# Grouped-query attention of block 2: the score tiles of two heads in turn, scored together on two halves of TensorE's rows

## The chip, the cores and the metric

The kernel runs on one core of a Trainium2 chip, in float32. The metric is the device time of one execution in microseconds (us). The kernel before took 2878.69 us (median of 3 runs, 2877.79 to 2880.61).

## The reference

Two transformer blocks run one after the other, on 512 tokens of width 1024; the second also has 256 context tokens. The change touches one attention of block 2: eight query heads of width 64 that share two heads of keys and values. Cut to what matters:

```
qb = rmsnorm(gq.reshape(lead + (GQA_HEADS, GQA_DIM)), qg_gain)        # 8 heads of 64
kb = rmsnorm(gk.reshape(lead + (GQA_KV_HEADS, GQA_DIM)), kg_gain)     # 2 heads of 64
...
def joint_dense_attention(q, k, v, kc, vc):       # the 512 tokens attend to context and tokens
    kk = jnp.concatenate([kc, k], axis=1)
    vv = jnp.concatenate([vc, v], axis=1)
    def block(qi):
        sc = jnp.einsum('bqkgd,bnkd->bkgqn', qi, kk) * (d ** -0.5)
        p = jax.nn.softmax(sc, axis=-1)
        return jnp.einsum('bkgqn,bnkd->bqkgd', p, vv)
```

The 256 context tokens attend among themselves in the same manner.

## The kernel before

The program is written engine by engine, with semaphores placed by hand, and falls into stages between which all engines meet. The stage of this change holds the grouped-query attention and, as a *filler* between its steps, the projections, norms and rotations of the first four heads of the latent attention (`pe_latent`, `dve_latent`, `act_latent`), which the next stage needs. The order on each engine is the order in which `pe_attention`, `dve_attention` and `act_attention` write it; no scheduler moves anything.

`dense(8, ...)` (L2464) makes the work list. A *unit* is one score tile: 128 queries of one head against all the keys it sees. Heads go in four couples (2m, 2m+1). For each couple there is a *main* group of 8 units (four query tiles of the first head, then four of the second, 768 keys each) and a *late* group of 4 units (two context tiles of each head, 256 keys each): 48 units in the stage, 32 of them main. Queries of an even head lie on partitions 0 to 63 of `QT`, those of an odd head on 64 to 127, and the keys lie on both halves of `KT`.

One unit x runs through the engines so:

- TensorE `score(x)` (L2331): one matmul of 512 keys and one of 256 into the double bank `PP[x % 2]`, with 64 rows. In float32 every matmul stands in the trace as two records with a weight load each. It waits until the exponential of unit x-2 has read that bank.
- VectorE `soften(x)` (L2386, L2391): the row maximum over 768 (or 256) columns, and its negative.
- ScalarE `exponentials(x)` (L2436): the exponential with the row sum, from `PP[x % 2]` into `PB`.
- VectorE `scale(x)` (L2402, L2404): the reciprocal of the sum, and the product with it.
- TensorE `turn_probs(x)` (L222): six (or two) transposes of 128x128 into `PP[2]`, which is one buffer: it waits until ScalarE has copied unit x-1 out of it.
- ScalarE `copy_probs(x)` (L2446): the copy from `PP[2]` to SBUF.
- When a group's probabilities are all there, TensorE `values` (L2352) makes the products with the values, two heads at once on the two halves of the array's columns, and VectorE (L2411) multiplies the gate by them. `Heads` (L2301) hands these products out two at a time to later units (`A.sums`).

TensorE's loop has score(x+1), a filler step, the values due at x, turn_probs(x-1), a filler step. So the score of the next unit is under way while VectorE and ScalarE work on this one. VectorE has soften(x+1), filler, scale(x), filler; ScalarE has exponentials(x), filler, copy_probs(x-1), filler. A filler step is one item of `latent_order`, in the same order on all engines: for each token tile a product of 384 columns (`q`) and one of 512 (`kv`), both into the one bank `PS[7]`, a square root on ScalarE with two loads of its function table for each two tiles, then many small steps of norm and rotation on VectorE, and four transposes of 96 for q and for k.

Of the kernel before, what the change touches and what calls it, by code (L numbers as in the profile page):

```python
# [95 lines left out]
def emit(nc, D, out, ctx):  # L96
# [13 lines left out]
    PP = [ctx.enter_context(nc.psum_tensor(f"ps{i}", [128, 1024], F32)) for i in range(4)]  # L110
# [44 lines left out]
    pe, dve, act, pool = [count(n + "_step") for n in ("pe", "dve", "act", "pool")]  # L155
# [4 lines left out]
    done, bank, read = {}, {}, {}  # L160
# [79 lines left out]
    class Block:  # L240


        def __init__(self, col, *parts, again=False, kept=False):
            self.col, self.parts = col, parts

            self.again, self.kept = again, kept
# [75 lines left out]
    ab = kp(D["ab_w_in_2"][0])  # L322
# [669 lines left out]
    def steps(filler, n=1):  # L992
        for _ in range(n):
            next(filler, None)
# [1056 lines left out]
    def whole(filler):  # L2051
        for _ in filler:
            pass
# [247 lines left out]
    class Heads:  # L2301


        def __init__(self, tag, groups, rate):
            self.tag, self.groups, self.units = tag, groups, []
            for g, grp in enumerate(groups):
                for n, u in enumerate(grp[0]):
                    self.units.append((g, n == len(grp[0]) - 1) + u)
            self.sums = {}
            todo = []  # L2310
            for x, u in enumerate(self.units):

                self.sums[x], todo = todo[:rate], todo[rate:]
                if x and self.units[x - 1][1]:
                    todo += self.of(x - 1)
            self.sums["end"] = todo + self.of(len(self.units) - 1)
# [5 lines left out]
    def pe_attention(e, A, PB, filler, rate):  # L2322
        exped, scaled, copied, taken_ = [signal(n) for n in ("exped", "scaled", "probs_copied", "values_taken")]
        units = A.units

        def score(x):
            g, end, q, ks = units[x][:4]
            if x >= 2:
                e.wait_ge(*exped.at(x - 1))
            for k, at in ks:  # L2330
                m = e.matmul(PP[x % 2][:, at:at + k.shape[1]], q, k, start=True, stop=True)  # L2331
            m.then_inc(*pe.up())
            done[A.tag, "score", x] = pe.now()

        def turn_probs(x):
            n = units[x][5]
            e.wait_ge(*scaled.at(x + 1))
            if x:
                e.wait_ge(*copied.at(x))
            transposes(e, [(PP[2][:, k * 128:k * 128 + 128], PB[:, x % 2, k * 128:k * 128 + 128]) for k in range(n // 128)]).then_inc(*pe.up())  # L2340
            done[A.tag, "turn", x] = pe.now()

        def values(sums):

            for g, j, x, k, v, c0, c1 in sums:
                bufs, vals = A.groups[g][1], A.groups[g][2]
                if j == 0:
                    e.wait_ge(*copied.at(x + 1))
                    if g:
                        e.wait_ge(*taken_.at(g))  # L2350
                for a in range(2):
                    m = e.matmul(PS[6][64 * a:64 * a + 64, c0:c1], v[a], bufs[a][:, k, c0:c1], start=(j == 0), stop=(j == len(vals) - 1))  # L2352
                if j == len(vals) - 1:
                    m.then_inc(*pe.up())
                    done[A.tag, "values", g] = pe.now()

        score(0)
        for x in range(len(units)):
            if x + 1 < len(units):
                score(x + 1)  # L2360
            steps(filler, rate)
            values(A.sums[x])
            if x:
                turn_probs(x - 1)
            steps(filler, rate)
        turn_probs(len(units) - 1)
        values(A.sums["end"])
        whole(filler)

    def dve_attention(e, A, PB, filler, rate):  # L2370
        units = A.units

        def masks(x):
            p = PP[x % 2]
            for n, (m, at) in enumerate(units[x][6]):
                e.wait_ge(*(dve.now() if n else done[A.tag, "score", x]))
                e.tensor_tensor(p[:, at:at + 128], p[:, at:at + 128], m, ALU.add).then_inc(*dve.up())  # L2377

        def soften(x):
            lo, n, sink = units[x][4], units[x][5], units[x][7]  # L2380
            m = sb[:, x % 2 * 8:x % 2 * 8 + 8]
            e.wait_ge(*done[A.tag, "score", x])
            e.wait_ge(*dve.now())
            if x >= 2:
                e.wait_ge(*signal("scaled").at(x - 1))
            e.tensor_reduce(m[:, 0:1], PP[x % 2][:, lo:lo + n], AX.X, ALU.max).then_inc(*dve.up())  # L2386
            e.wait_ge(*dve.now())
            if sink is not None:
                e.tensor_scalar(m[:, 0:1], m[:, 0:1], sink, -1.0, ALU.max, ALU.mult).then_inc(*dve.up())
            else:  # L2390
                e.tensor_scalar(m[:, 0:1], m[:, 0:1], -1.0, None, ALU.mult).then_inc(*dve.up())  # L2391
            done[A.tag, "max", x] = dve.now()

        def scale(x):
            n, sink = units[x][5], units[x][7]
            m = sb[:, x % 2 * 8:x % 2 * 8 + 8]
            e.wait_ge(*signal("exped").at(x + 1))
            if sink is not None:
                e.wait_ge(*signal("sunk").at(x + 1))
                e.tensor_tensor(m[:, 1:2], m[:, 1:2], m[:, 2:3], ALU.add).then_inc(*dve.up())  # L2400
                e.wait_ge(*dve.now())
            e.reciprocal(m[:, 3:4], m[:, 1:2]).then_inc(*dve.up())  # L2402
            e.wait_ge(*dve.now())
            e.tensor_scalar(PB[:, x % 2, 0:n], PB[:, x % 2, 0:n], m[:, 3:4], None, ALU.mult).then_inc(*signal("scaled").up())  # L2404

        def values(sums):
            for g, j, x, k, v, c0, c1 in sums:
                if j == len(A.groups[g][2]) - 1:
                    n, dst = A.groups[g][3], A.groups[g][4]
                    e.wait_ge(*done[A.tag, "values", g])  # L2410
                    e.tensor_tensor(dst, dst, PS[6][:, 0:n], ALU.mult).then_inc(*signal("values_taken").up())  # L2411

        masks(0)
        soften(0)
        for x in range(len(units)):

            if x + 1 < len(units):
                masks(x + 1)
                soften(x + 1)
            steps(filler, rate)  # L2420
            scale(x)
            values(A.sums[x])
            steps(filler, rate)
        values(A.sums["end"])
        whole(filler)

    def act_attention(e, A, PB, filler, rate):
        units = A.units

        def exponentials(x):  # L2430
            lo, n, sink = units[x][4], units[x][5], units[x][7]
            m = sb[:, x % 2 * 8:x % 2 * 8 + 8]
            e.wait_ge(*done[A.tag, "max", x])
            if x >= 2:
                e.wait_ge(*done[A.tag, "turn", x - 2])
            e.activation(PB[:, x % 2, 0:n], PP[x % 2][:, lo:lo + n], ACT.Exp, bias=m[:, 0:1], accum_out=m[:, 1:2]).then_inc(*signal("exped").up())  # L2436
            if sink is not None:
                e.activation(m[:, 2:3], m[:, 0:1], ACT.Exp, bias=sink).then_inc(*signal("sunk").up())

        def copy_probs(x):  # L2440
            g, end, c, places, a = units[x][0], units[x][1], units[x][8], units[x][9], units[x][10]
            e.wait_ge(*done[A.tag, "turn", x])
            if g >= 2:
                e.wait_ge(*done[A.tag, "values", g - 2])
            for k0, k1, to in places:
                m = e.activation(A.groups[g][1][a][:, to:to + k1 - k0, c * 128:c * 128 + 128],  # L2446
                                 PP[2][:, k0 * 128:k1 * 128].rearrange("p (k n) -> p k n", n=128), ACT.Copy)
            m.then_inc(*signal("probs_copied").up())

        for x in range(len(units)):  # L2450
            exponentials(x)
            steps(filler, rate)
            if x:
                copy_probs(x - 1)
            steps(filler, rate)
        copy_probs(len(units) - 1)
        whole(filler)
# [150 lines left out]
    def pool_latent(e, hh):  # L2608
        for what, i in latent_order():
            if what == "kv":  # L2610
                if i >= 2:
# [2 lines left out]
                              KR[:, i, :].unsqueeze(1).to_broadcast([128, 4, 32])).then_inc(*signal("kr_copied").up())  # L2614

    gqa = Heads("gqa", dense(8, lambda h: QT[half(h), h // 2, :], lambda h: KT[half(h), h // 4, :],
                             lambda h, k: GKV[:, k, 128 + 64 * (h // 4):192 + 64 * (h // 4)], 4), 2)
    pe_attention(nc.tensor, gqa, PB, pe_latent(nc.tensor, 0), 1)
    dve_attention(nc.vector, gqa, PB, dve_latent(nc.vector, 0), 1)
    act_attention(nc.scalar, gqa, PB, act_latent(nc.scalar, 0), 1)  # L2620
# [257 lines left out]
```

## Time and profile before

| | |
|---|---|
| Time, median of 3 runs | 2878.69 us (2877.79 to 2880.61) |
| The profiled execution: its own time, its span | 2879.6 us, 2878.4 us |
| TensorE matmul busy | 2589.5 us, 90% of the span |
| VectorE, ScalarE busy | 995.8 us (35%), 562.5 us (20%) |
| Granted TensorE clock, mean over the span | 0.94 |
| The stage of the change | 2073.6 to 2256.1 us, 182.5 us |
| in it: TensorE, VectorE, ScalarE busy | 169.25, 112.64, 91.15 us |
| in it: granted clock, DMA share | 0.84, 0.00 |

Times are from the start of the span. Busy times of matmuls are a little too long, since a record runs on past the start of the next one; what TensorE needs for a piece is read from the start of its first matmul to the start of the next piece. A clock of 1.00 is 2.4 GHz and 0.50 is 1.2 GHz; no other level occurs. "Idle before" names the engine and line whose signal ended the idle time.

### The profile page before, as it was taken

Reading aid. Unit: us, or ns where it says so; the run is one execution under the profiler, and the core shown is the slowest. Engines: PE = TensorE matmul, PEld = TensorE weight load, DVE = VectorE, ACT = ScalarE, POOL = GpSimd, SP = SyncE. Lnnn points to the kernel's source line nnn. Section 1 sums busy time; section 2 is a strip of 40 time slices with the busy share of each in tenths; the row PEclk is TensorE's granted clock in tenths of the full one; section 3 lists DMA queues with packets and bytes.
Section 4 is the critical chain, followed back from the end, with each engine's and each line's share of the span. In section 5 each row is a group of like instructions: output and inputs, shape, how many; then the busy total and the mean of one; then the engine's idle time right before and its main releaser. Section 6 shows DMA issues by size and latency. Waiting matters only on the chain. (4 is left out here: it accounts for less than half of the span.)

```text
span 2878.4 us, 27051 instructions
## 1 busy us (share of the span) xinstructions
PE 2589.5 (90%) x10307; PEld 1262.8 (44%) x10307; DVE 995.8 (35%) x2127; ACT 562.5 (20%) x1274; POOL 170.0 (6%) x316
## 2 busy tenths in 40 slices
PE   5979778875999999999999999798999789999998
PEld 2534646342334334444343333365544444454453
DVE  2665344333121111111121111345066665332272
ACT  1355322010000000000000000121255544210250
POOL 0000514101000000000000000200000000000000
PEclk8999999976999999999999999899988999999889
DMA  9110185605899999958948999810000002022000
GB/s 324 63 59 30 60 327 180 267 33 195 361 401 414 416 404 417 414 229 323 382 186 354 411 419 417 324 59 26 29 1 1 1 1 81 19 84 86 31 1 29
DMA packets 143354, 565.43 MB, mean 196 GB/s; under 512 B 15429, under 2 KB 36158, under 8 KB 105202
## 3 DMA queue, kind: packets, MB, share of 16 engines
q1 hardware_dynamic: 127336, 515.97, 45.7%
q0 software_dynamic: 12992, 42.51, 3.9%
q10 hardware_dynamic: 2890, 5.13, 0.5%
q8 instruction: 85, 1.39, 0.2%
q14 instruction: 51, 0.42, 0.0%
HBM read 537.24 MB, written 26.35 MB: 196 GB/s over the span
## 5 line engine op out<-in xcount | busy, mean ns | idle before, releaser
L1585 PE MATMUL ps<-ring,mem 128*32 128x512 f32 (+2 forms) x1888 | 517.8, 603 | 10.4 <-issue 10.4
L216 PE MATMUL ps<-ring,mem 128*128 128x512 f32 (+5 forms) x1136 | 398.1, 508 | 29.9 <-DVEq L181 15.0
L216 PE MATMUL ps<-mem,ring 128*128 128x512 f32 (+1 forms) x1056 | 422.0, 559 | 2.6 <-DVE mem L736 1.6
L1585 PEld LDWEIGHTS ps<-ring,mem 128*32 128x32 f32 (+2 forms) x1888 | 189.9, 147 | 278.1 <-issue 278.1
L216 PEld LDWEIGHTS ps<-ring,mem 128*128 128x128 f32 x1136 | 202.9, 197 | 210.2 <-issue 178.8
L216 PEld LDWEIGHTS ps<-mem,ring 128*128 128x128 f32 x1056 | 201.5, 192 | 213.1 <-issue 204.4
L1614 PE MATMUL ps<-ring,mem 128*32 128x512 f32 (+2 forms) x1056 | 270.5, 603 | 9.2 <-issue 9.2
L222 PE MATMUL ps<-mem 128*128 128x128 f32 (+3 forms) x1203 | 193.5, 294 | 85.2 <-DMA mem<-h_rows,mem 14.2
L222 PEld LDWEIGHTS ps<-mem 128*128 128x128 f32 (+3 forms) x1203 | 145.5, 148 | 210.5 <-issue 138.2
L1585 PE MATMUL ps<-mem 128*32 128x512 f32 (+2 forms) x800 | 234.8, 596 | 2.4 <-issue 2.4
L1646 DVE COPY mem<-ps 128x512 f32<-128x512 f32 x48 | 33.2, 692 | 505.9 <-PE ps L222 505.9
L1654 ACT ACTIVATE mem<-mem 128x512 f32<-128x512 f32 x48 | 28.1, 632 | 784.2 <-DVE mem L1630 784.2
L1622 DVE COPY mem<-ps 128x512 f32<-128x512 f32 x48 | 33.3, 693 | 410.8 <-PE ps L222 410.8
L1614 PEld LDWEIGHTS ps<-ring,mem 128*32 128x32 f32 (+2 forms) x1056 | 99.8, 141 | 155.3 <-issue 155.3
L2331 PE MATMUL ps<-ring 64*128 64x256 f32 (+4 forms) x328 | 133.7, 531 | 14.8 <-ACT mem L2436 4.6
L2386 DVE TENSOR_REDUCE mem<-ps 128x1 f32<-128x768 f32 (+3 forms) x128 | 99.1, 774 | 132.3 <-PE ps L2331 125.4
L1585 PEld LDWEIGHTS ps<-mem 128*32 128x32 f32 (+2 forms) x800 | 84.1, 145 | 108.7 <-issue 108.7
L1614 PE MATMUL ps<-mem 128*128 128x512 f32 (+2 forms) x288 | 122.1, 604 | 0.0
L2446 ACT ACTIVATE ring<-ps 128x768 f32<-128x768 f32 (+2 forms) x128 | 75.4, 602 | 121.7 <-PE ps L222 121.5
L2099 ACT ACTIVATE mem<-ps 128x512 f32<-128x512 f32 (+2 forms) x68 | 33.0, 487 | 329.5 <-PE ps L216 329.5
L2331 PEld LDWEIGHTS ps<-ring 64*128 64x128 f32 (+1 forms) x328 | 62.9, 215 | 64.6 <-issue 51.0
L1661 ACT ACTIVATE mem<-ps 128x512 f32<-128x512 f32 x48 | 26.1, 595 | 294.0 <-PE ps L1614 294.0
(374 smaller groups left out, 2373.9 us busy)
## 6 DMA issues: line engine op xcount, KB each, us to landing
ring<-in_w_up SPq DMA_DIRECT2D x91, 2048.0 KB, 15.9
ring<-in_w_down SPq DMA_DIRECT2D x47, 2048.0 KB, 22.4
mem<-in_w_up SPq DMA_DIRECT2D x37, 2048.0 KB, 18.3
mem<-in_w_down SPq DMA_DIRECT2D x17, 2048.0 KB, 20.6
ring<-in_w_ada SPq DMA_DIRECT2D x12, 2048.0 KB, 7.5
ring<-in_mod_w SPq DMA_DIRECT2D x8, 2048.0 KB, 10.4
ring<-in_cd_w_in SPq DMA_DIRECT2D x6, 2048.0 KB, 7.9
y_rows<-mem POOLq DMA_DIRECT2D x23, 512.0 KB, 8.0
```

The lines of the kernel that those rows point to most:

```text
L216: i = e.matmul(o, l, r, start=(n == 0), stop=(n == len(pairs) - 1))
L222: r = e.transpose(o, i, ident[0:k, 0:k])
L1585: m = e.matmul(PS[n][c0:c0 + rows, :], XGT[:, u, k * 128 + c0:k * 128 + c0 + rows], wt[:, kk, n * 512:n * 512 + 512], start=False, stop=(k ...
L1614: m = e.matmul(PS[6 + n][c0:c0 + rows, :], ACTT[:, k * 128 + c0:k * 128 + c0 + rows], wt[:, kk, n * 512:n * 512 + 512], start=False, stop= ...
L1622: e.tensor_copy(XGT[:, i % 2, hh * 512:hh * 512 + 512], PS[4]).then_inc(L.x_copied, 1)
L1646: e.tensor_copy(ACTT[:, hh * 512:hh * 512 + 512], PS[5]).then_inc(L.a_copied, 1)
L1654: e.activation(SG[:, c], T1[:, c], ACT.Sigmoid, scale=1.702).then_inc(L.gate, 1)
L1661: e.activation(Y[:, i % 2, n * 512:n * 512 + 512], PS[6 + n], ACT.Copy).then_inc(L.y_copied, 1)
L2099: e.activation(dst, bank[key][:, 0:n], func).then_inc(*empties(key))
L2331: m = e.matmul(PP[x % 2][:, at:at + k.shape[1]], q, k, start=True, stop=True)
L2386: e.tensor_reduce(m[:, 0:1], PP[x % 2][:, lo:lo + n], AX.X, ALU.max).then_inc(*dve.up())
L2446: m = e.activation(A.groups[g][1][a][:, to:to + k1 - k0, c * 128:c * 128 + 128], PP[2][:, k0 * 128:k1 * 128].rearrange("p (k n) -> p k n", ...
```

## The change

The units of a group are put in another order for this one attention (`side_by_side=True`, in block 2's grouped-query stage alone): first head's tile 0, second head's tile 0, first head's tile 1, and so on. Each loop then takes two units, a *pair*, at a time: 24 pairs, 16 of main units and 8 of late ones. TensorE scores both units of a pair together, one on rows 0 to 63 into `PP[0]` and one on rows 64 to 127 into `PP[1]`, once the exponentials of both units of the pair before are done. VectorE makes both maxima; ScalarE makes both exponentials. No instruction is added or removed; each engine still takes four filler steps for two units. The other attentions keep their loops.

```diff
+        def __init__(self, tag, groups, rate, side_by_side=False):
...
+                if side_by_side:
+                    us = [u for ab in zip(us[:half], us[half:]) for u in ab]
@@ pe_attention @@
+        def scores(x):
+            if x:
+                e.wait_ge(*exped.at(x))
+            for (k0, at), (k1, _) in zip(units[x][3], units[x + 1][3]):
+                e.matmul(PP[0][:, at:at + k0.shape[1]], units[x][2], k0, start=True, stop=True)
+                m = e.matmul(PP[1][:, at:at + k1.shape[1]], units[x + 1][2], k1, start=True, stop=True)
+            m.then_inc(*pe.up())
+            done[A.tag, "score", x] = done[A.tag, "score", x + 1] = pe.now()
+
+        if A.side_by_side:
+            for x in range(0, len(units), 2):
+                scores(x)
+                if x:
+                    turn_probs(x - 2)
+                steps(filler, rate)
+                values(A.sums[x])
+                steps(filler, rate)
+                if x:
+                    turn_probs(x - 1)
+                steps(filler, rate)
+                values(A.sums[x + 1])
+                steps(filler, rate)
@@ dve_attention @@
+        if A.side_by_side:
+            for x in range(0, len(units), 2):
+                for u in (x, x + 1):
+                    masks(u)
+                    soften(u)
+                steps(filler, rate)
+                scale(x)
+                values(A.sums[x])
+                steps(filler, rate)
+                scale(x + 1)
+                values(A.sums[x + 1])
+                steps(filler, 2 * rate)
@@ act_attention @@
+        if A.side_by_side:
+            for x in range(0, len(units), 2):
+                if x:
+                    copy_probs(x - 2)
+                steps(filler, rate)
+                exponentials(x)
+                steps(filler, rate)
+                exponentials(x + 1)
+                steps(filler, rate)
+                if x:
+                    copy_probs(x - 1)
+                steps(filler, rate)
```

How this moves instructions, at three places. First TensorE in main units of the first group with no filler product between them (the score line is L2331 before and L2365, L2366 after; L222 are the transposes). Before:

```order
L2331 MATMUL ps<-ring 128x512
L2331 MATMUL ps<-ring 128x256
L222 MATMUL ps<-mem 128x128 x6
L2331 MATMUL ps<-ring 128x512
L2331 MATMUL ps<-ring 128x256
L222 MATMUL ps<-mem 128x128 x6
```

After:

```order
L2365 MATMUL ps<-ring 128x512
L2366 MATMUL ps<-ring 128x512
L2365 MATMUL ps<-ring 128x256
L2366 MATMUL ps<-ring 128x256
L222 MATMUL ps<-mem 128x128 x12
```

Scores and transposes took turns unit by unit; now four score matmuls stand together, the two heads in turn, and then the twelve transposes of the pair before.

VectorE where the second pair begins, with the maximum (L2386, now L2417), its negative (L2391, L2422), the reciprocal (L2402, L2433), the product (L2404, L2435) and, as filler, the mean (L2561, L2623), its inverse (L2565, L2627) and two steps of a norm (L2027, L2030). Before:

```order
L2386 TENSOR_REDUCE mem<-ps 128x1
L2391 TENSOR_SCALAR mem<-mem 128x1
L2561 TENSOR_SCALAR mem<-mem 128x16
L2402 RECIPROCAL mem<-mem 128x1
L2404 TENSOR_SCALAR mem<-mem 128x768
L2565 RECIPROCAL mem<-mem 128x16
L2027 TENSOR_TENSOR mem<-mem 128x384
L2386 TENSOR_REDUCE mem<-ps 128x1
L2391 TENSOR_SCALAR mem<-mem 128x1
L2030 SCALAR_TENSOR_TENSOR mem<-mem 128x384
L2402 RECIPROCAL mem<-mem 128x1
L2404 TENSOR_SCALAR mem<-mem 128x768
```

After:

```order
L2417 TENSOR_REDUCE mem<-ps 128x1
L2422 TENSOR_SCALAR mem<-mem 128x1
L2417 TENSOR_REDUCE mem<-ps 128x1
L2422 TENSOR_SCALAR mem<-mem 128x1
L2623 TENSOR_SCALAR mem<-mem 128x16
L2433 RECIPROCAL mem<-mem 128x1
L2435 TENSOR_SCALAR mem<-mem 128x768
L2627 RECIPROCAL mem<-mem 128x16
L2027 TENSOR_TENSOR mem<-mem 128x384
L2433 RECIPROCAL mem<-mem 128x1
L2435 TENSOR_SCALAR mem<-mem 128x768
L2030 SCALAR_TENSOR_TENSOR mem<-mem 128x384
```

The second maximum now stands ahead of the first unit's filler step and product.

TensorE in the late pairs of the first group after the change, with the values of the main group between (L2356):

```order
L2365 MATMUL ps<-ring 128x256
L2366 MATMUL ps<-ring 128x256
L222 MATMUL ps<-mem 128x128 x12
L2356 MATMUL ps<-ring,mem 64x512 x4
L2365 MATMUL ps<-ring 128x256
L2366 MATMUL ps<-ring 128x256
L222 MATMUL ps<-mem 128x128 x2
L2356 MATMUL ps<-ring,mem 64x512 x4
L222 MATMUL ps<-mem 128x128 x2
L2356 MATMUL ps<-ring,mem 64x512 x4
```

The first piece of the values follows the last transposes of the main group directly; before, one late score stood ahead of it.

## Rows read from the trace of the kernel before

**Rows 1.** Stretches: length; busy us of PE, PEld, DVE, ACT, POOL; clock; DMA share.
```profile
2073.60:2256.10 182.50, 169.25 (x609) 80.89 (x609) 112.64 (x302) 91.15 (x190) 2.09 (x6) 0.84 0.00 1
2073.90:2094.40 20.50, 19.92 (x32) 8.87 (x31) 8.05 (x16) 5.60 (x10) 0.20 (x1) 0.50 0.00 0
...
2155.90:2169.50 13.60, 13.60 (x38) 6.79 (x37) 8.27 (x31) 5.20 (x13) 0.00 (x0) 0.50 0.00 1
...
2152.40:2155.80 3.40, 1.27 (x6) 0.62 (x5) 2.33 (x7) 3.37 (x6) 0.00 (x0) 1.00 0.00 0
```

**Rows 2.** The same for L2331 (the scores) alone, over the stage.
```profile
2073.60:2256.10 182.50, 69.20 (x161) 29.55 (x161) 0.84 0.00 1
```

**Rows 3.** Timeline at 2.4 GHz, main units, no filler: start, length, engine, line.
```profile
2229.24 1.55 PE L2331 MATMUL ps<-ring 64*128 64x512 f32 x4
...
2230.73 0.87 PE L222 MATMUL ps<-mem 128*128 128x128 f32 x6
2230.84 0.96 DVE L2386 TENSOR_REDUCE mem<-ps 128x1 f32<-128x768 f32 x1 [1.67 <-PE ps L2331]
...
2231.53 1.55 PE L2331 MATMUL ps<-ring 64*128 64x512 f32 x4
2231.64 0.81 ACT L2446 ACTIVATE ring<-ps 128x768 f32<-128x768 f32 x1 [0.60 <-PE ps L222]
2231.83 0.15 DVE L2391 TENSOR_SCALAR mem<-mem 128x1 f32<-128x1 f32 x1
...
2232.34 0.90 ACT L2436 ACTIVATE mem<-ps,mem 128x768 f32<-128x768 f32 x1
```

**Rows 4.** Timeline, the stage's first negated maximum and what it releases.
```profile
2077.40 0.15 DVE L2391 TENSOR_SCALAR mem<-mem 128x1 f32<-128x1 f32 x1
2077.65 1.28 ACT L2436 ACT_TABLE_LOAD   x1 [4.34 <-DVE mem L2391]
```

**Rows 5.** Timeline, an exponential and the score that waited for it.
```profile
2100.76 0.90 ACT L2436 ACTIVATE mem<-ps,mem 128x768 f32<-128x768 f32 x1
...
2101.81 1.55 PE L2331 MATMUL ps<-ring 64*128 64x512 f32 x4 [1.37 <-ACT mem L2436]
```

**Rows 6.** Timeline, VectorE through one main unit with two filler steps.
```profile
2105.95 0.96 DVE L2386 TENSOR_REDUCE mem<-ps 128x1 f32<-128x768 f32 x1
...
2106.94 0.15 DVE L2391 TENSOR_SCALAR mem<-mem 128x1 f32<-128x1 f32 x1
2107.13 0.56 DVE L2027 TENSOR_TENSOR mem<-mem 128x384 f32<-128x384 f32 x1
...
2108.98 0.96 DVE L2386 TENSOR_REDUCE mem<-ps 128x1 f32<-128x768 f32 x1
```

**Rows 7.** Timeline at 1.2 GHz: a score and what follows it; transposes and their copy.
```profile
2085.88 2.93 PE L2331 MATMUL ps<-ring 64*128 64x512 f32 x4
...
2088.74 2.93 PE L216 MATMUL ps<-ring,mem 128*128 128x384 f32 x4
...
2111.31 1.42 PE L222 MATMUL ps<-mem 128*128 128x128 f32 x6 [1.32 <-DVE mem L2404]
...
2112.77 0.81 ACT L2446 ACTIVATE ring<-ps 128x768 f32<-128x768 f32 x1 [1.62 <-PE ps L222]
```

**Rows 8.** Timeline at 2.4 GHz: the filler's two products, and a piece of values.
```profile
2138.86 1.56 PE L216 MATMUL ps<-ring,mem 128*128 128x384 f32 x4
...
2141.83 1.98 PE L216 MATMUL ps<-ring,mem 128*128 128x512 f32 x4
...
2219.25 1.94 PE L2352 MATMUL ps<-ring,mem 128*64 128x512 f32 x8
```

**Rows 9.** Timeline, the score held up behind a filler square root.
```profile
2154.91 2.03 PE L2331 MATMUL ps<-ring 64*128 64x512 f32 x4 [2.13 <-ACT mem L2436]
```

**Rows 10.** Block 1's 64-row scores: records within 126.600 to 126.607, then to 126.612.
```profile
L604 PE MATMUL ps<-mem x2: 373/375/377, 126.4 to 126.6; 64*128 64x256 f32 x2
...
L604 PE MATMUL ps<-mem x3: 373/373/377, 126.4 to 126.6; 64*128 64x256 f32 x2, 64*128 64x128 f32 x1
```

More of the change, by code:

```diff
@@ L2301, in emit @@
     class Heads:
-        def __init__(self, tag, groups, rate):
-            self.tag, self.groups, self.units = tag, groups, []
+        def __init__(self, tag, groups, rate, side_by_side=False):
+            self.tag, self.groups, self.units, self.side_by_side = tag, groups, [], side_by_side
             for g, grp in enumerate(groups):
-                for n, u in enumerate(grp[0]):
-                    self.units.append((g, n == len(grp[0]) - 1) + u)
+                us, half = grp[0], len(grp[0]) // 2
+                if side_by_side:
+                    us = [u for ab in zip(us[:half], us[half:]) for u in ab]
+                for n, u in enumerate(us):
+                    self.units.append((g, n == len(us) - 1) + u)
             self.sums = {}
@@ L2355, in values @@
                     done[A.tag, "values", g] = pe.now()
+        def scores(x):
[19 more added lines that the diff above has]
+                steps(filler, rate)
+            turn_probs(len(units) - 2)
+            turn_probs(len(units) - 1)
+            values(A.sums["end"])
+            whole(filler)
+            return
         score(0)
@@ L2411, in values @@
                     e.tensor_tensor(dst, dst, PS[6][:, 0:n], ALU.mult).then_inc(*signal("values_taken").up())
+        if A.side_by_side:
[10 more added lines that the diff above has]
+                steps(filler, 2 * rate)
+            values(A.sums["end"])
+            whole(filler)
+            return
         masks(0)
@@ L2448, in copy_probs @@
             m.then_inc(*signal("probs_copied").up())
+        if A.side_by_side:
[10 more added lines that the diff above has]
+                steps(filler, rate)
+            copy_probs(len(units) - 2)
+            copy_probs(len(units) - 1)
+            whole(filler)
+            return
         for x in range(len(units)):
@@ L2616, in emit @@
     gqa = Heads("gqa", dense(8, lambda h: QT[half(h), h // 2, :], lambda h: KT[half(h), h // 4, :],
-                             lambda h, k: GKV[:, k, 128 + 64 * (h // 4):192 + 64 * (h // 4)], 4), 2)
+                             lambda h, k: GKV[:, k, 128 + 64 * (h // 4):192 + 64 * (h // 4)], 4), 2, True)
     pe_attention(nc.tensor, gqa, PB, pe_latent(nc.tensor, 0), 1)
```

## The prediction

> **What bounds the kernel now.** I read the engines' shares first, then the stretches of the stage, the groups by line inside it, and the timeline of single units. TensorE is busy in 169.25 of the stage's 182.5 us, VectorE in 112.64, ScalarE in 91.15, and no DMA plays a part [rows 1]. So the stage is TensorE's, and the scores are its largest piece, 69.20 us of busy time [rows 2]. The granted clock is the other thing to read there: 0.84 on average, which is 1.2 GHz for (1 - 0.84) x 2 = 32% of the stage, some 58 us; the first 20.5 us are all at 1.2 GHz with TensorE busy in 19.92, and the stretch at 1.2 GHz from 2155.9 on follows one at 2.4 GHz in which TensorE was busy in only 1.27 of 3.40 us [rows 1].
>
> In main units without filler the units follow one another every 2231.53 - 2229.24 = 2.29 us, which is the score, 1.49 us up to the transposes, and the transposes, 0.80 us up to the next score [rows 3]. TensorE never waits there: maximum and exponential of one unit are made while it scores the next. With norm steps as filler it is VectorE that sets the pace, 2108.98 - 2105.95 = 3.03 us a unit [rows 6].
>
> **The change, part by part.**
>
> *Scores.* If the two heads' matmuls run at once, a main pair needs one score time and not two: 1.49 us less at 2.4 GHz, 2088.74 - 2085.88 = 2.86 us less at 1.2 GHz [rows 3, 7]. The difference of the two, 1.37 us, is what goes by the clock at 2.4 GHz, and 0.12 is fixed. A late pair has 256 columns for 768: 1.37 / 3 + 0.12, some 0.6 us less. As TensorE work alone that is 16 x 1.49 + 8 x 0.6 = 28.6 us at 2.4 GHz. Whether they run at once: in block 1 the trace has matmuls of 64 rows for different heads, and a second record starts within 12 ns of one of another shape, 256 columns and 128 [rows 10]. In the program these two are an even head's last and the next head's first, on different row halves. I take them as concurrent. The Trainium skill (TensorE: Matmul & The Clock Gate, section "Part 3: Packing small matmuls", under what overlaps and what doesn't) has it that matmuls start and end strictly in program order. Each float32 matmul is two passes; if the passes of one matmul stood together in that order, the other head's first pass could start only beside the second pass of the first head's, one pass late. By that rule the sum would be 9 us larger; it is one of the rivals below, and the trace speaks against it.
>
> *The new wait.* scores(x) now needs the exponentials of both units before it, and both banks `PP[0]` and `PP[1]` are then filled at once, so no score is under way while maxima and exponentials are made. A plain main pair at 2.4 GHz, from score to score: score to maximum 1.60, maximum to negative 0.99 [rows 3], to the second maximum 0.19 [rows 6], again 0.99, negative to exponential 0.25 [rows 4], exponential to the next score 1.05 [rows 5]: 5.07 us. The first unit's path does not come later: transposes at 1.49, copy 0.91 on, exponential 0.70 on, so at 3.10, and the second 0.9 after it at 4.0, beside 4.02. TensorE has 1.49 + 2 x 0.80 = 3.1 us of work in it, so it is idle for 2.0. Before, two such units took 4.58: **each plain pair loses 0.5 us** at 2.4 GHz. Where norm steps fill VectorE, its 3.03 us a unit give 6.06 a pair before and after; with the short rotation steps among them I take 5.6, between 5.07 and 6.06.
>
> *The other pairs,* each walked through the same way, at 2.4 GHz. A filler product takes TensorE 1.5 us (384 columns) or 1.85 (512), a piece of values 1.87, which are the records less the 0.1 that they run on past the next start [rows 8]; a copy out of `PS[7]` delays the next product by 0.5 to 0.8, an estimate from the copy of 0.81 out of `PP[2]` [rows 3].
> - First pair: scores 2.9 at 1.2 GHz, four products 7.1, waits for their bank 2.1: 12.1 us, if the clock rises soon after the scores, because the scores then load all rows and a product follows at once. If it stays at 1.2 GHz through all four products, as it did before [rows 1], 18.1. I take 12.1.
> - Pairs with the square root: the pair's chain plus a table load of 1.28 us [rows 4] each way and the root; before, the score was held up 2.13 us there [rows 9]. 8.6 us for pair 2. Where products of the next tiles stand in the same pair the exponentials on ScalarE wait behind their copies: 10.5 and 9.7 in group 2, 9.4 and 8.2 in group 3, with 8.9 for the late pair after it.
> - First late pair of a group: the values need copy_probs of unit 7, which ScalarE now does only after both exponentials: 3.3 to the copy, 0.9, then 1.87 of values: 6.1 us. Second late pair: two pieces of values and little else: 5.1.
> - First main pair of the next group, in which the late values wait for the same reason: 5.3 to the copy's end, 1.1 values: 6.4, and with the four transposes of filler 8.0 (7.7).
>
> Groups: 12.1 + 8.6 + 5.6 + 5.6 + 6.1 + 5.1 = 43.1; 8.0 + 10.5 + 9.7 + 5.6 + 6.1 + 5.1 = 45.0; 6.4 + 6.0 + 9.4 + 8.2 + 8.9 + 5.1 = 44.0; 7.7 + 3 x 5.07 + 6.1 + 5.1 + 3.6 for the tail = 37.7. Sum **169.8 us at 2.4 GHz**, against 182.5 with its 58 us at 1.2 GHz.
>
> *The clock.* A plain pair at 1.2 GHz: transposes at 2.86, copy 1.46 later, exponential 0.70 on, the second 0.9 on, next score 1.05 on: 6.97 us [rows 3, 5, 7]. Pieces of values and products double. Over all kinds a pair of 7.0 us (169.8 / 24) becomes about 9.3, an estimate: one third more. After its first stretch the stage had about 38 of 162 us at 1.2 GHz before. TensorE is now idle 2.0 of 5.07 us in the plain pair, 2.5 of 5.6 beside norm steps and 4 to 5 us on end in the three pairs with a square root; a gap of that kind stands ahead of the fall in rows 1. So I take more than before: 30% of the pairs' work. That costs 0.3 x 157.7 x 1/3 = 15.8 us. The stage then takes 185.6 us, **3.1 more than before**. Bounds: no fall after the first pair, 169.8; half of the work at 1.2 GHz and a slow first pair, 169.8 + 6.0 + 26.3 = 202.
>
> What costs nothing: VectorE's and ScalarE's work is the same in number, and no DMA waits on the stage. The next stage starts as before.
>
> The profiled execution took 2879.6 us and the median is 0.9 less; 2879.6 + 3.1 = 2882.7 against the profile, about 2882 as a median.
>
> **The rivals.**
> 1. *Slower, by the clock and the wait for both exponentials.* The place is the main pairs, where TensorE idles 2 us of 5 to 6; the price is a third on each pair done at 1.2 GHz, and 6.0 if the first products stay there too. For it: busy shares such as 3.1 of 5.07 are new for the plain units, which ran without a gap. Against: two heads at once load all rows, which may let the clock rise again sooner. With 45% of the work at 1.2 GHz and the slow first pair: 169.8 + 6.0 + 23.7 = 199.5, so 2896. It decides from 188.3 us on: 35% of the work, or 24% with the slow first pair.
> 2. *Faster.* The clock rises early in the stage and falls only at the square roots: a tenth of the work at 1.2 GHz gives 175.1 us, 7.4 less, 2871. For it: the first 20.5 us at 1.2 GHz hold the scores with half the rows idle. Against: the gaps above.
> 3. *The change doesn't do what it says:* the second head runs one pass behind the first. A pass of 512 columns is a third of the 1.37 us, 0.46, and one of 256 is 0.23: 16 x 0.46 + 8 x 0.23 = 9.2 us on the sum, 2891. With no overlap at all it would be 28.6, 2910. Rows 10 speak against both.
>
> **How the numbers follow.** A measurement of this kernel can tell 0.2%, 5.8 us, from no change. Forecast 0.42 (within 0.2%), rival 1 0.33, rival 2 0.20, rival 3 0.05. So faster 0.20, same 0.42, slower 0.38. The range goes from a little under rival 2 to rival 1: 2869 to 2896; the forecast's own is 2874 to 2885.
>
> **What would show it.** Score records of the two heads starting within some 10 ns, 1.5 us from a main score's start to the transposes; TensorE idle before the score, ended by the exponential (L2482), in nearly every main pair, about 1 us; plain pairs 5.1 us apart; a mean clock of 0.75 to 0.8 in the stage; the values of a main group waiting for L2492. The forecast is wrong if the stage is at 2.4 GHz for 90% of its time, if plain pairs follow at under 4.6 us, or if the second head's records start a pass later.

## The result, and the profile after

The changed kernel took 2895.49 us (median of 5 runs, 2892.59 to 2902.17) against 2877.79 for the kernel before on the same chip (5 runs, 2877.15 to 2880.61): 1.0063 times as long, 95% interval 1.0048 to 1.0078. That is 17.7 us slower. The profiled execution has a span of 2894.3 us, 15.9 more than before. Of them 14.0 arise in the stage of the change, 3.7 stood there before it began, on the same instructions, and 1.8 were won back after it. The 3.7 are chance: in the runs below the stage begins anywhere from 2070.1 to 2079.3 us.

The length of a stage is read from one profile and is less sure than a time. The loops of before, where nothing else was changed that should matter, took 182.5, 178.2 (e1) and 179.2 us (e9), so a few us between two stages may be chance, mostly of the clock. The paired loops took 196.5 us twice (here and in e2).

The stretches of the profile after: the whole stage; 3.4 us in which TensorE does nothing, because the exponential waits behind a filler square root; and the stretch at 1.2 GHz that follows (length; busy us of PE, PEld, DVE, ACT, POOL; clock; DMA share; GB/s).

```profile
2077.30:2273.80 196.50, 143.91 (x609) 70.81 (x609) 115.59 (x302) 90.78 (x190) 1.75 (x7) 0.80 0.00 1
...
2152.90:2156.30 3.40, 0.00 (x0) 0.00 (x0) 1.40 (x4) 3.34 (x6) 0.00 (x0) 1.00 0.00 0
...
2156.30:2176.80 20.50, 14.96 (x49) 7.60 (x50) 10.95 (x35) 7.57 (x15) 0.00 (x0) 0.50 0.00 0
```

Against [rows 1]: TensorE is busy for 143.9 us and not 169.25, 25 us less, as meant. But the stage takes 196.5 us for 182.5, so TensorE idles 53 us for 13. The clock is 0.80 for 0.84, which is 78 us at 1.2 GHz for 58. VectorE has 3 us more than before, ScalarE the same.

Who waited for whom in the stage, after (engine, line, what it waited for: us in total, times, longest):

```profile
PE ps L2365 <- ACT mem L2482: 16.6, 9, 4.8
PE ps L222 <- ACT ring L2492: 14.6, 15, 1.6
...
ACT mem L2482 <- PE ps L222: 10.8, 9, 1.4
PE ps L2356 <- ACT ring L2492: 10.7, 8, 2.4
```

Two of these were forecast: the score for the exponential (L2482) and the values for the copy (L2492). Two were not: the second transposes wait for the copy of the first ones, and the *exponential waits for the transposes*. The timeline of one plain main pair at 2.4 GHz shows it, and answers to [rows 3]:

```profile
2242.58 0.69 PE L2365 MATMUL ps<-ring 64*128 64x512 f32 x1 [1.14 <-ACT mem L2482]
2242.59 0.69 PE L2366 MATMUL ps<-ring 64*128 64x512 f32 x1
...
2244.07 0.87 PE L222 MATMUL ps<-mem 128*128 128x128 f32 x6
2244.19 0.96 DVE L2417 TENSOR_REDUCE mem<-ps 128x1 f32<-128x768 f32 x1 [0.81 <-PE ps L2366]
2244.98 0.81 ACT L2492 ACTIVATE ring<-ps 128x768 f32<-128x768 f32 x1 [1.75 <-PE ps L222]
...
2245.69 0.90 ACT L2482 ACTIVATE mem<-ps,mem 128x768 f32<-128x768 f32 x1
2245.94 0.85 PE L222 MATMUL ps<-mem 128*128 128x128 f32 x6 [0.99 <-ACT ring L2492]
2246.41 0.15 DVE L2422 TENSOR_SCALAR mem<-mem 128x1 f32<-128x1 f32 x1
...
2246.88 0.90 ACT L2482 ACTIVATE mem<-ps,mem 128x768 f32<-128x768 f32 x1 [0.20 <-DVE mem L2433]
...
2247.93 0.72 PE L2365 MATMUL ps<-ring 64*128 64x512 f32 x1 [1.14 <-ACT mem L2482]
```

The two heads' scores start 10 ns apart, the transposes come 1.49 us after the score and the maximum 1.61: as forecast. The second exponential starts at 2246.88, though its negated maximum began at 2246.41 (0.25 us was enough in [rows 4]) and ScalarE had been idle for 0.20. The trace puts this wait down to a VectorE line that it does not depend on in the program. What the program makes it wait for are the transposes of 2245.94, which read the same one of the two probability buffers and end at 2246.79, just ahead of it; e3 puts this to the test. Pair to pair is 5.35 us, for 5.07 forecast and 4.58 for two units before. In the first late pair of a group the same wait stands ahead of the values:

```profile
2115.45 1.51 PE L222 MATMUL ps<-mem 128*128 128x128 f32 x6 [0.99 <-ACT ring L2492]
...
2117.06 0.48 ACT L2482 ACTIVATE mem<-ps,mem 128x256 f32<-128x256 f32 x1 [1.30 <-PE ps L222]
...
2117.53 0.80 ACT L2492 ACTIVATE ring<-ps 128x768 f32<-128x768 f32 x1
...
2118.38 3.68 PE L2356 MATMUL ps<-ring,mem 128*64 128x512 f32 x8 [1.42 <-ACT ring L2492]
```

Transposes, exponential, copy, values: one behind the other.

### The profile page after: what moved, and what is told of

The parts are those of the page before. It is cut to its first block and busy times, and to the rows that moved or that the text cites. A ratio compares the mean times of both kernels' runs of the same rounds, so it can differ in the third digit from the quotient of the medians.

```text
span 2894.3 us, 27051 instructions
## 1 busy us (share of the span) xinstructions
PE 2572.3 (89%) x10307; PEld 1254.1 (43%) x10307; DVE 998.3 (34%) x2127; ACT 562.8 (19%) x1274; POOL 170.1 (6%) x316
## 5 line engine op out<-in xcount | busy, mean ns | idle before, releaser
L222 PE MATMUL ps<-mem 128*128 128x128 f32 (+3 forms) x1203 | 197.7, 299 | 97.9 <-ACT ring L2492 16.9
L222 PEld LDWEIGHTS ps<-mem 128*128 128x128 f32 (+3 forms) x1203 | 148.8, 150 | 216.8 <-issue 153.9
L2417 DVE TENSOR_REDUCE mem<-ps 128x1 f32<-128x768 f32 (+3 forms) x128 | 99.1, 774 | 121.9 <-PE ps L2366 93.5
L2492 ACT ACTIVATE ring<-ps 128x768 f32<-128x768 f32 (+2 forms) x128 | 75.4, 602 | 132.5 <-PE ps L222 132.5
L2356 PE MATMUL ps<-ring,mem 128*64 128x512 f32 (+2 forms) x304 | 76.2, 628 | 15.7 <-ACT ring L2492 15.7
L2482 ACT ACTIVATE mem<-ps,mem 128x768 f32<-128x768 f32 (+1 forms) x96 | 72.8, 758 | 25.8 <-DVE mem L2422 13.6
```

Of the source, the lines that this page charges most:

```text
L222: r = e.transpose(o, i, ident[0:k, 0:k])
```

## The experiments

Theory A: the paired loops lose by their waits (both exponentials before a score, the exponential for the transposes), at any clock. Theory B: they lose by the clock, which falls because TensorE waits. Theory C: the two heads' scores don't really overlap, or the new order of the units costs. A run's stage is counted from its first score to the first score of the next stage. Each ratio is against the kernel before in the same batch of runs.

### e1: the new order of the units alone

In the three attention loops:

```diff
-        if A.side_by_side:
+        if False:
             for x in range(0, len(units), 2):
```

> The units in their new order (heads in turn), but the loops of before: one score at a time, a unit ahead. If the loss comes from the paired loops (no score under way during maxima and exponentials, and the clock that follows), this runs as before: 2878 us, within 4. If the order of the units itself costs (the probabilities of a group are complete only at its last unit on both heads), it lands nearer the change: 2888 or more.

0.9989 of before, interval 0.9975 to 1.0004; the stage takes 178.2 us. The order of the units costs nothing that can be measured, so the loss is the paired loops'. One part of theory C is out.

### e2: one head's score after the other

```diff
-            for (k0, at), (k1, _) in zip(units[x][3], units[x + 1][3]):
-                e.matmul(PP[0][:, at:at + k0.shape[1]], units[x][2], k0, start=True, stop=True)
-                m = e.matmul(PP[1][:, at:at + k1.shape[1]], units[x + 1][2], k1, start=True, stop=True)
+            for u in (x, x + 1):
+                for k, at in units[u][3]:
+                    m = e.matmul(PP[u % 2][:, at:at + k.shape[1]], units[u][2], k, start=True, stop=True)
```

> The paired loops, but TensorE scores the whole first unit and then the whole second. If the two heads' records really run at once in the change, this loses it: one more score time in the chain of each pair, 16 x 1.37 + 8 x 0.46 = 25.6 us at 2.4 GHz, less what a busier TensorE gets back in clock: 2908 to 2922 us. If the overlap is worth nothing: 2895.

1.0049, interval 1.0031 to 1.0067: as the change. The stage takes 196.5 us like the change's, and its 24 pairs start at the same distances within 0.15 us. That is the number written for "the overlap is worth nothing", but the trace shows why it may not be read so. L2366 within 2238.38 to 2238.41, and the timeline there:

```profile
L2366 PEld LDWEIGHTS ps<-ring x2: 183/183/183, 2238.4 to 2238.4; 64*128 64x128 f32 x2
L2366 PE MATMUL ps<-ring x2: 693/693/693, 2238.4 to 2238.4; 64*128 64x512 f32 x2
```

```profile
2238.39 1.57 PE L2366 MATMUL ps<-ring 64*128 64x512 f32 x8 [1.14 <-ACT mem L2482]
...
2239.88 0.87 PE L222 MATMUL ps<-mem 128*128 128x128 f32 x6
```

Two records of 512 columns begin within 30 ns. They cannot be one head's two, which start 0.5 us apart on their rows; so the second is the other head's, although in the program three more records of the first head stand between them. All eight are through in 1.5 us. So what is written for the other half of the rows overtakes. The edit changed next to nothing, so the run tells nothing of the overlap's worth; e5 does.

### e3: four probability buffers

The grouped-query stage alone uses memory that is free then (the second half of `GQ`'s place, which the next stage takes for keys):

```diff
-            if x >= 2:
-                e.wait_ge(*done[A.tag, "turn", x - 2])
-            e.activation(PB[:, x % 2, 0:n], ...
+            if x >= PB.shape[1]:
+                e.wait_ge(*done[A.tag, "turn", x - PB.shape[1]])
+            e.activation(PB[:, x % PB.shape[1], 0:n], ...
...
+    PB4 = gq_.rearrange("p (a n) -> p a n", n=768)
```

> The change with four buffers for the probabilities for two. In the profile after, the second exponential of a pair starts 0.94 us after the transposes of the unit two before it, also where its maximum has long been there. Theory A: this second wait (the transposes wait for the copy of the unit before, the exponential for the transposes) costs 0.3 us in a plain pair at 2.4 GHz, 0.9 at 1.2 GHz and 1 us or more in the first late pair of each group: 2884 to 2890 us. Rival: only the chain of two maxima and two exponentials counts, and the buffer is hidden: 2895.

1.0032, interval 1.0019 to 1.0046, about half of the change's loss: 9 us less than the change, or 6 if e2 of the same batch is taken for it. The stage takes 185.8 us, 10.7 less, but in the fastest of twelve runs (2877.56 us, for a median of 2884.45), so 10.7 is likely too much. On ScalarE the two exponentials now follow each other in 0.91 us, for 1.19:

```profile
2233.97 0.90 ACT L2482 ACTIVATE mem<-ps,mem 128x768 f32<-128x768 f32 x1
2234.75 0.20 ACT L2482 ACTIVATION_READ_ACCUMULATOR mem<-ps,mem 128x1 f32 x1
2234.88 0.90 ACT L2482 ACTIVATE mem<-ps,mem 128x768 f32<-128x768 f32 x1
```

The wait is there and costs. Part of the gain is clock: 0.85 for 0.80, 55 us at 1.2 GHz for 78.

### e4: the change with TensorE kept busy

```diff
+        def warm(n):
+            if n and given[0]:
+                e.wait_ge(*taken_.at(given[0]))
+            for _ in range(n):
+                e.matmul(PS[6][:, 0:256], ident, QT[:, 0, 0:256], start=True, stop=True)
...
+    WARM = {2: (2, 8), 4: (2, 2), 6: (2, 2), 8: (0, 0), 16: (0, 8), 18: (2, 2), 26: (0, 1), 32: (3, 0), 38: (2, 2), 40: (2, 2), 42: (2, 2)}
...
                 values(A.sums[x])
                 steps(filler, rate)
+                warm(WARM.get(x, (0, 0))[0])
...
                 values(A.sums[x + 1])
                 steps(filler, rate)
+                warm(WARM.get(x, (0, 0))[1])
...
         pe_twice_t(e, "kt", lambda i: GKV[:, i, 0:128], 2, range(6))
+        o = next_bank(e, "warm")
+        for n in range(4):
+            m = e.matmul(o, ident, HT[:, 0, 0:512], start=True, stop=True)
+        m.then_inc(*empties("warm"))
```

> The change with spare matmuls (identity by 256 columns, into a bank that holds nothing then) where TensorE waits: four 512-column ones before the stage, 2 and 2 in plain main pairs, 8 in two pairs with a square root. They leave every other instruction as it is. If the clock is what makes the pairs slow, the stage runs at a mean clock over 0.92 and takes 172 to 180 us for 196.5: 2870 to 2880 us. Rival: the pairs are bound by the chain of both exponentials alone and the spare work only gets in the way: 2895 or more.

1.0002, interval 0.9989 to 1.0014. The clock comes to 0.94 and the stage to 179.4 us:

```profile
2072.10:2251.50 179.40, 144.25 (x701) 76.39 (x701) 114.71 (x302) 91.20 (x190) 1.78 (x7) 0.94 0.00 1
```

These are 46 spare matmuls of 256 columns in the stage and four of 512 ahead of it. Work that is thrown away won 17 us. So the clock matters; whether it explains the *difference* to before needs the same done to before (e8).

### e5: the overlap barred

As e2, with a matmul of all 128 rows between the two heads (the second score overwrites its result):

```diff
             for u in (x, x + 1):
+                if u > x:
+                    at = units[u][3][0][1]
+                    e.matmul(PP[1][:, at:at + 32], ident, QT[:, 0, 0:32], start=True, stop=True)
```

> As e2, with one matmul of all 128 rows and 32 columns between the first unit's score and the second's (its result is overwritten by the second score). In e2 TensorE ran the two heads' records side by side although they were written one unit after the other; the matmul on all rows should end that. If the overlap is real and worth what the score takes, each main pair now has two score times in its chain: 16 x 1.5 + 8 x 0.6 = 29 us more at 2.4 GHz than the change, some of it given back by the clock since TensorE is busier: the stage 205 to 225 us, the time 1.008 to 1.018 of before. If the overlap is worth nothing: as the change, 1.006, the stage 196.

1.0308, interval 1.0285 to 1.0331; the stage takes 268.4 us at a clock of 0.68. TensorE at 2.4 GHz:

```profile
2250.18 1.55 PE L2369 MATMUL ps<-ring 64*128 64x512 f32 x4
2251.67 0.41 PE L2367 MATMUL ps<-ring,mem 128*128 128x32 f32 x2
2252.01 1.55 PE L2369 MATMUL ps<-ring 64*128 64x512 f32 x4
2253.49 0.88 PE L222 MATMUL ps<-mem 128*128 128x128 f32 x6
```

3.3 us from the first score to the transposes, for 1.5. So the overlap is real, and theory C is out altogether. (The small matmul covers all rows and also writes the second head's bank; which of the two bars the overlap was not separated.) The size was missed: 72 us more than the change for 10 to 30. The direction of the clock was wrong too: TensorE is busier, 218 us, and yet had (1 - 0.68) x 2 x 268 = 172 us at 1.2 GHz. So the clock does not go by busy time alone. What the overlap is worth at 2.4 GHz can be read from a plain pair that runs there as a whole:

```profile
2286.35 1.55 PE L2369 MATMUL ps<-ring 64*128 64x512 f32 x4
...
2293.51 0.69 PE L2369 MATMUL ps<-ring 64*128 64x512 f32 x1 [1.14 <-ACT mem L2485]
```

7.16 us for 5.35, so 1.8 a pair. In a late pair the second head's score begins 1.0 us after the first's. As an estimate, 16 x 1.8 + 8 x 1.0 = 37 of the 72 us are the overlap, and the rest is clock.

### e6: four buffers and kept busy

e3 and e4 together.

> e3 and e4 together. If the two waits (clock, and exponential for the transposes out of the double buffer) are what separates the change from its sum at 2.4 GHz, their gains add up in part: the stage 168 to 174 us, the time 0.994 to 0.998 of before. Rival: what is left is the chain of both exponentials, and one of the two hides the other: the stage 178 or more, the time 1.000.

0.9999, interval 0.9988 to 1.0009; the stage takes 175.8 us at 0.95, 3.6 less than e4. Neither expectation's stage holds it. The plain pair is now what the prediction's chain gave:

```profile
2225.38 0.69 PE L2372 MATMUL ps<-ring 64*128 64x512 f32 x1
...
2230.45 0.69 PE L2372 MATMUL ps<-ring 64*128 64x512 f32 x1
```

5.07 us, for 5.34 in e4. At a nearly held clock the buffer is worth 0.27 us in a plain pair and 3.6 us in the stage, of which a little may be clock or chance (17 us at 1.2 GHz for 21); in the whole time the two runs can't be told apart. So most of what e3 won came by way of the clock. And what is left, at a nearly full clock, is still not faster than before.

### e7: before, kept busy at the stage's start alone

The kernel before with only the last four lines of e4's edit.

> The kernel before with nothing but the four spare 512-column matmuls on TensorE between its last transposes and the stage, where it waits for ScalarE. If the clock at the stage's start (20.5 us at 1.2 GHz) hangs on that idle time, the stage starts at 2.4 GHz and gains about 9 us: 0.997 of before. Rival: the clock falls at the first wait anyway: 1.000.

0.9974, interval 0.9962 to 0.9986; the stage takes 171.3 us and begins at 2.4 GHz:

```profile
2079.30:2100.00 20.70, 17.55 (x57) 8.71 (x58) 14.57 (x32) 12.68 (x22) 0.49 (x2) 1.00 0.00 1
```

The 20.5 us at 1.2 GHz with which the stage of before begins [rows 1] hung on TensorE's idle time ahead of it. The clock still falls later, and the stage has 37.5 us at 1.2 GHz for 58.

### e8: before, kept busy in its waits too

```diff
+            if A.tag == "gqa" and WARM.get(x, 0):
+                if given[0]:
+                    e.wait_ge(*taken_.at(given[0]))
+                for _ in range(WARM[x]):
+                    e.matmul(PS[6][:, 0:256], ident, QT[:, 0, 0:256], start=True, stop=True)
             if x + 1 < len(units):
                 score(x + 1)
...
+    WARM = {4: 3, 8: 2, 9: 2, 18: 4, 33: 3, 32: 2}
```

> The kernel before with the spare matmuls at the start and at six places where TensorE waits in its stage (2 to 4 of 256 columns). If the clock is most of what the stage of before loses too, it keeps a mean clock over 0.95 and takes 156 to 165 us for 182.5: 0.990 to 0.994 of before, faster than any paired version. Rival: the spare work delays the scores as much as the clock gives: 0.998 to 1.002.

0.9932, interval 0.9916 to 0.9949: 2857.09 us for 2876.14, the fastest version here.

```profile
2075.00:2237.20 162.20, 150.92 (x640) 77.51 (x641) 112.61 (x302) 91.29 (x190) 2.09 (x6) 0.99 0.00 1
```

This is the run that decides between A and B. Keeping TensorE busy gives the loops of before 182.5 - 162.2 = 20.3 us and the paired loops 196.5 - 179.4 = 17.1. The clock costs both about the same (for before rather less, 16 to 20 us, if e1's and e9's stages of 178 and 179 us are its usual length). With it nearly held (0.99 and 0.94) the paired loops are 17 us slower, or some 13 if e4's remaining 21 us at 1.2 GHz are counted as an estimated loss of 5. The whole times say the same: e4 and e8 are 0.0070 of before apart, 20 us, and with those 5 taken off 15, where the change lost 17.7. So theory A is right about the difference between the two kernels, and theory B about what both of them lose.

### e9: before with four buffers

e3's edit in the kernel before.

> The kernel before with four probability buffers for two, nothing else. If the wait of an exponential for the transposes two units back is new with the paired loops, it hides nothing here: 1.000 of before, within 0.0015, the stage 182 within 3. If the double buffer held up the loops of before too, the stage gains some us as in e3: 0.997 or less.

1.0005, interval 0.9989 to 1.0021; its stage, from 2078.8 to 2258.0, takes 179.2 us, within what was expected. The double buffer held up nothing before; its wait is new with the paired loops.

### e10 to e12: all filler ahead of the attention

In each of the three attention functions:

```diff
     def pe_attention(e, A, PB, filler, rate):
+        if A.tag == "gqa":
+            whole(filler)
```

e10 has the loops of before, e11 the paired loops, e12 these with four buffers. All have the spare matmuls at the start; e11 and e12 also have 2 and 2 in the main pairs without values.

> The loops of before (with the spare matmuls at the stage's start), but all filler runs ahead of the attention. The last group of before, almost free of filler and at 2.4 GHz, took 38.3 us, so four should take some 153 us from the first score on, more where the clock falls. The time as a whole is worse than before, since nothing hides the filler; only the attention part, first score to the next stage, is compared with e11 and e12.

> The paired loops with all filler ahead of them, spare matmuls at the start and 2 and 2 in the main pairs without values. If what the paired loops lose at an equal clock (e4's 179 against e8's 162 us) comes from the filler, whose products wait for copies that stand on ScalarE between and behind the two exponentials, the loss is gone here: the attention part 148 to 156 us, within 4 us of e10's. If the chain of both maxima and both exponentials itself is slower, it shows without filler too: 8 us or more above e10.

> e11 with four probability buffers. Main pairs follow at 5.1 us for 5.35, and the first late pair is shorter: 4 to 8 us less than e11. If the buffer costs nothing without filler: as e11.

The attention part takes 140.6, 152.3 and 141.3 us; the times are 1.0130 (1.0113 to 1.0147), 1.0139 (1.0122 to 1.0156) and 1.0114 (1.0097 to 1.0131) of before. e10's first 41 us were at 1.2 GHz, so its total flatters the paired loops. e12 is 11 us below e11, more than the 4 to 8 expected, and its clock is higher: 16 us at 1.2 GHz for 27. One group of 12 units in each, the second. e10:

```profile
2192.80:2223.10 30.30, 29.12 (x130) 14.38 (x129) 19.70 (x51) 17.02 (x36) 0.00 (x0) 1.00 0.00 1
```

e11:

```profile
2182.60:2220.10 37.50, 30.80 (x156) 16.10 (x154) 20.48 (x50) 17.01 (x36) 0.00 (x0) 0.91 0.00 1
```

e12:

```profile
2185.70:2220.20 34.50, 29.13 (x154) 15.64 (x152) 20.38 (x50) 16.94 (x36) 0.00 (x0) 0.95 0.00 1
```

30.3, 37.5 and 34.5 us. My idea that the filler's copies behind the exponentials make the loss falls: without any filler the paired loops are 7.2 us a group slower, of which four buffers (and 0.04 of clock) take back 3.0. Some of the 7.2 is clock, 0.91 for 1.00: by the prediction's third, 6.8 us at 1.2 GHz cost about 1.7. The chain itself is slower. From score to score the six pairs of this group take 7.3, 6.0, 5.35, 5.35, 8.3 and 5.2 us in e11 and 6.8, 6.2, 5.07, 5.07, 6.2 and 5.1 in e12. So two plain pairs lose 0.77 us each against 4.58, and the first late pair, where values wait for a copy that comes behind both exponentials, gains most from four buffers (and from the clock, which had fallen there in e11). e10's expected 153 us was wrong too, and too high in spite of the low clock at first: the last group of before, from which I took it, still held some filler.

## Why the prediction was right, and where it was not

The prediction put "no measurable change" first, at 2882 us, with 2874 to 2885 as this forecast's own range and 2869 to 2896 as the range over the rivals. The median is 2895.5: inside the wide range, at its upper edge, and slower beyond doubt (1.0048 to 1.0078). So the first choice (0.42) failed, and rival 1 (0.33, 2896 us) came. Its number fits partly by luck: it stood for a stage of 199.5 us with 45% of the work at 1.2 GHz and the first products there too. The stage took 196.5, the first products ran at 2.4 GHz from 3.9 us on, some 36% of the work was at 1.2 (an estimate: 75 of the 78 us, less the prediction's third), and 3.7 us lay ahead of the stage by chance. Of the forecast's mechanism one half is confirmed.

**Scores.** Right. Main scores take 1.49 us up to the transposes and start 10 ns apart. TensorE's busy time fell by 25 us, for 28.6 worked out as work at 2.4 GHz; the profile has more of it at 1.2 GHz than before, where every record is longer. Rival 3 is out. The Trainium skill (TensorE: Matmul & The Clock Gate, section "Part 3: Packing small matmuls") says that matmuls are strictly first in, first out; e2 shows matmuls on other rows overtaking three records of the first head, so here the measurement decides against the rule. The price put on it, 9 us, was due neither for this order nor for the other.

**The new wait.** Right in kind. TensorE idles ahead of the score in each plain pair, ended by L2482. The chain of 5.07 us is met to the hundredth in e6, with four buffers, but the change itself takes 5.35. The step that failed is "the first unit's path does not come later": it followed the copy to the first exponential and did not go on to the second transposes, which wait for that copy and release the second exponential. At 2.4 GHz that is 0.28 us in a plain pair. At 1.2 GHz it is more: the pair at 2157.30, all of it at 1.2 GHz, took 8.05 us to the next score, and the one at 2097.51, with 4.2 us at 1.2 GHz, took 7.3, for 6.97 forecast. e4 against e6 puts the buffer at 3.6 us of the stage with the clock nearly held, and e3 against the change at 6 to 10.7 with what the clock adds.

**The sum at 2.4 GHz.** 169.8 us was forecast. No run held the clock fully; e4 took 179.4 with (1 - 0.94) x 2 x 179 = 21 us at 1.2 GHz. By the prediction's own figure, a third more on the work, those 21 us cost about 5, which leaves some 174 us as an estimate. e4 also began at 2.4 GHz, and its first pair took 10.6 us where the sum has 12.1, so the sum is 5 to 6 us too low. The buffer's 3.6 is the larger part of that; the rest stays open. The single pairs of the change came close: first pair 12.3 us for 12.1, second 8.0 for 8.6, the two with products behind the waits 11.7 and 9.6 for 10.5 and 9.7.

**The clock.** The term was 15.8 us for 30% of the work at 1.2 GHz, which makes 66 of 185.6 us, 36% of the time. The profile has 78 of 196.5 us there, 40%. The gap between 196.5 and 174 is 22 us, or 21 without the 1.5 that the sum already holds for the first pair, so the term was a quarter too small, 5 us. The stage took 10.9 us more than the 185.6 forecast, about half of it from the sum and half from this term. The first products behaved as chosen: the clock rose at 2081.2, 3.9 us into the stage.

**What the comparison left out.** The prediction took the paired loops apart into a sum at 2.4 GHz and a clock term, 169.8 and 15.8 us, but not the loops of before, whose 182.5 us it took whole. It never worked out before's own sum at 2.4 GHz, which e8 shows as 162.2 us. Set against that, its numbers say that the waits cost 7.6 us and that the clock gives back 4.5; neither stands in it. Rival 1 named two causes, the clock and the wait for both exponentials. With the clock taken off on both sides (about 174 against 161 to 162 us) the waits cost some 13 us of the 14.0. The clock's share in the *difference* is small: it costs some 22 us here and 21 there, or 17 if the 178 us of e1 are taken for before. That tells where the gain of 25 us of TensorE work went: it was traded for a loop in which no score is under way while maxima and exponentials are made, and TensorE's idle time grew by 39 us. That the missing second set of score banks makes this chain is read from the timeline (5.07 us a pair with four buffers, 4.58 before); no run gave the paired loops such banks. Rival 2, the fast clock, did not occur.

**What stays open.** Why e5 has so much of its time at 1.2 GHz; how the rest of e11's 7.2 us a group, beyond the plain pairs' 0.77 each and the clock, splits among the pairs in which values wait for a copy; and whether four score banks would make the paired loops the faster ones.

## What to carry to other kernels

Halving a piece of an engine's work is worth nothing if the merge takes away the step that ran ahead. Check first whether there are buffers for two pairs: here that means four probability buffers (e3) and, not tried, twice the score banks. Follow each buffer's release to the second user. Compare both versions at the same clock, and work out the old one's sum at that clock as well. And where an engine's idle time lowers its clock, a few matmuls whose results nobody reads, put where it would wait anyway, can do more than a reordering: twenty of them gave 0.68% here (e8).

## What the runs showed of the hardware

- Matmuls on different halves of the rows do not start strictly in the order in which the program has them. With two heads' scores written one after the other, four records on rows 0 to 63 and then four on rows 64 to 127, the second head's first record starts within 30 ns of the first head's (e2), and the next piece starts as early as in the change. One small matmul on all rows between them, into the second head's bank, ends this (e5): 3.3 us for 1.5.
- The busy share of a stretch does not tell its clock. In before TensorE was busy in all of the 13.6 us from 2155.9, at 1.2 GHz throughout [rows 1]. e5 kept TensorE busy in 218 of 268 us, 81%, at a mean clock of 0.68; e4 in 144 of 179 us, 80%, at 0.94. In e5 the scores ran on half of the rows one after the other; in e4 both halves worked at once and full-row matmuls filled the gaps.
- Four matmuls of 512 columns ahead of the stage, where TensorE had been idle for 4 us, kept the first 21 us of the stage at 2.4 GHz (e7), where before had 20.5 us at 1.2 GHz: 11.2 us less in the stage, 7.5 in the whole time.
